# A bidirectional scan's two directions: added by VectorE for every head instead of by GpSimd for half of them and by TensorE for the rest

## The chip, the cores and the metric

One core of a Trainium2 chip runs the whole program in one launch. The metric is the device time of that launch in microseconds (us), the median of several runs. The engines are TensorE (PE in the profile, PEld for its weight loads), VectorE (DVE), ScalarE (ACT), GpSimd (POOL) and the DMA queue of SyncE (SP). They run side by side and wait for each other through semaphores.

## The reference, cut to what matters

Two layers of an encoder trunk on 512 positions of width 1024, in float32. The part that counts here is a Mamba-2 scan of 16 heads of width 64, run forwards and backwards in 4 chunks of 128 positions, the two directions summed:

```python
seg = a_cs[:, :, :, None] - a_cs[:, :, None, :]
decay = jnp.exp(jnp.where(lower, seg, -jnp.inf))
cb = jnp.einsum('bclgn,bcsgn->bclsg', Cc, Bc)
y_diag = jnp.einsum('bclsge,bcsgep->bclgep', cb[..., None] * decay, X)
...
y = y_fwd + y_bwd + d_skip.astype(f32)[:, None] * xs
```

For one head and one chunk, y_diag of both directions is (G_fwd + G_bwd) X, with G = cb * decay a 128x128 matrix for each direction and X (the head's 64 columns of inputs, 128 positions) the same in both. So the two matrices may be added first and multiplied once, or multiplied one by one into the same accumulator. Around the scan stand projections, attention, a short convolution and a gated feed-forward part.

## The kernel before, in words

Activations lie transposed, 128 features by 512 positions. Every weight matrix is cut into chunks of 128x1024, and each chunk becomes one tile of output in one of the eight PSUM banks. Float32 accuracy comes from a split: ScalarE writes a chunk's high part (L528), VectorE or GpSimd the low part, raw minus high (L834, L433), and TensorE makes three products a block (L1158 to L1160), 24 for a chunk. Raw, high and low parts have two buffers each. So chunk n+2 gets its high part when TensorE has used chunk n, then its low part, and its raw buffer is refilled by SP when that low part is done. TensorE starts chunk n+2 only when its whole low part is there.

The stage that the change touches is a list of slots written out by hand (SLOTS, L69): slots 0 to 11 are the short convolution's chunks, 12 to 19 the chunks of z (the gate), 20 to 27 the first half of the output projection. All engines go through the same list, each in its own order. In slot s TensorE first makes the tile of s and then the pieces of the scan that are due there; VectorE makes the low part of chunk s+2 (`low_after`, L829); in this stage all low parts are VectorE's. GROUP_AT, SEG_AT, WEIGH_AT and PAIR_AT (L112 to L115) say in which slot each piece of the scan is due; heads 0 to 7 have slots 3 to 12, heads 8 to 15 slots 14 to 23.

For a head h:

- SP copies 2x512 numbers to all partitions (`head_rows`, L350) into one of four buffers, `head_e(h)` = HEAD_E[h % 4]: two are in sb_e, one is sb_e_third, one is sb_squares. For h of 4 and more this waits for the products of the pair that used the buffer.
- VectorE subtracts a column, 8 instructions of 128x128 (`seg`, L905), ScalarE takes the exponential (L602), and VectorE multiplies both directions by CB from PSUM (`weigh`, L911, in slot WEIGH_AT). `g_done` counts these.
- For even h, GpSimd adds the second direction to the first (`add_directions`, L464); `gs_done` counts these.

Pair t is heads 2t and 2t+1, in slots 6, 8, 10, 12 and 17, 19, 21, 23. There TensorE makes `from_states` (L1336) and `within` (L1322): for an even head one product a chunk of positions, for an odd head two that accumulate, one for each direction. The even head's output goes to partitions 0 to 63 of a bank, the odd head's to 64 to 127. Before it TensorE waits for the even head's sum and for the odd head's `weigh`, which VectorE makes one slot earlier, in front of that slot's low part. In the pair's own slot VectorE combines the result behind its low part (`combine`, L915 to L923); SP's copies of the exponentials for the next pair (`pair_exps`, L370) and of the next heads' rows stand in the same queue as the weight loads (L333).

GpSimd has in this stage: the low part of the short convolution's output (L489, slots 2, 5, 8, 11), the scaled inputs of the states (L458), the adds of L464, the backward part (L468) and the gate (L473). A z tile is moved out of its bank by VectorE behind the slot's low part and `combine` (L1085), and TensorE's tile two slots later needs that bank.

Of the kernel before, what the change touches and what calls it, by code (L numbers as in the profile page):

```python
# [142 lines left out]
def build_trunk(nc, a):  # L143
# [18 lines left out]
    def sem(name, per=0):  # L162
        return Count(ctx.enter_context(nc.semaphore(name)), per, now)
# [68 lines left out]
    def bank(i):  # L232
# [43 lines left out]
    cb_mm, cb_done, xs_done, st_mm, sin_done = sem("cb_mm", 2), sem("cb_done", 4), sem("xs_done", 12), sem("st_mm", 12), sem("sin_done", 8)  # L276
    seg_done, e_done, g_done, y_mm = (
        sem(n, SSD_HEADS) for n in ("seg_done", "e_done", "g_done", "y_mm"))
    gs_done = sem("gs_done", SSD_HEADS // 2)
    yo_mm, y_read, t_read, z_copied, y_comb = (sem(n, 8) for n in ("yo_mm", "y_read", "t_read", "z_copied", "y_comb"))  # L280
    z_done = sem("z_done", 2)
    ff_tap, ff_silu, ff_hi, ff_lo = sem("ff_tap", 2 * FF_T), sem("ff_silu_done", FF_T), sem("ff_hi_done", FF_T), sem("ff_lo_done", FF_T)
# [8 lines left out]
    def head_e(h):  # L291

        return HEAD_E[h % 4]
# [130 lines left out]
    @block.gpsimd  # L424
    def _(pool):
        g = nc.gpsimd

        def w_low(n):
            pool.wait_ge(w_hi.handle, n + 1)
            if n % NCH == POS["dt", 0]:  # L430
                g.tensor_tensor(dt_parts(n, 1), dt_raw(n), dt_parts(n, 0).bitcast(F32), ALU.subtract).then_inc(w_lo.handle, 1)
                return
            g.tensor_tensor(WLO[:, n % 2, :], W[:, n % 2, :], WHI[:, n % 2, :].bitcast(F32), ALU.subtract).then_inc(w_lo.handle, 1)  # L433

        def low_after(kind, i):

            n = now[0] * NCH + POS[kind, i] + 2
            if (kind, i) == ("o2", 0):
                pool.wait_ge(w_lo.handle, n)
            if n < DEPTH * NCH:  # L440
                w_low(n)

        def sum_squares(grp):

            pool.wait_ge(*y_sq.at(4 * grp + 4))
            g.tensor_tensor(SQS[:, 0:2, :], SQS[:, 0:2, :], SQS[:, 2:4, :], ALU.add).then_inc(y_tree.handle, 1)
            pool.wait_ge(*y_tree.at(2 * grp + 1))
            g.tensor_tensor(SQS[:, 0, :], SQS[:, 0, :], SQS[:, 1, :], ALU.add).then_inc(y_tree.handle, 1)

        def scale_states(n):  # L450
            grp, j = n // 6, n % 6
            d, c = direction_chunk(j)
            col = column(d, 8 * grp)
            pool.wait_ge(*ws_done.at(1))
            pool.wait_ge(*tok_copied.at(5 * grp + 5))
            if j >= 2:
                pool.wait_ge(*st_mm.at(n - 1))
            g.tensor_tensor(SQ[:, j % 2, :].rearrange("p (h e) -> p h e", e=64), XT[:, c, :].rearrange("p (h e) -> p h e", e=64),  # L458
                            WS[:, c, col:col + 8].unsqueeze(2).to_broadcast([P, 8, 64]), ALU.mult).then_inc(xs_done.handle, 1)

        def add_directions(h):

            pool.wait_ge(*g_done.at(h + 1))
            g.tensor_tensor(head_e(h)[:, 0, :], head_e(h)[:, 0, :], head_e(h)[:, 1, :], ALU.add).then_inc(gs_done.handle, 1)  # L464

        def add_backward(t):
            pool.wait_ge(*y_read.at(t + 1))
            g.tensor_tensor(XC[:, t, 0:SEQ - P], XC[:, t, 0:SEQ - P], T[:, 1, 0:SEQ - P], ALU.add).then_inc(t_read.handle, 1)  # L468

        def gate(t):  # L470
            pool.wait_ge(*t_read.at(t + 1))
            pool.wait_ge(*z_done.at(t // 4 + 1))
            g.tensor_tensor(XC[:, t, :], XC[:, t, :], Z[:, t % 4, :], ALU.mult).then_inc(y_comb.handle, 1)  # L473

        w_low(0)
        w_low(1)
        for layer in range(DEPTH):
            now[0] = layer
            for pos in range(POS["sc", 0]):
                low_after(*CHUNKS[pos])  # L480
                if layer == 0 and CHUNKS[pos] == ("qk", 2):
                    pool.wait_ge(bias_row.handle, 2)
                    g.dma_start(scratch[:, :, :], rm["bias_row"][:, :].unsqueeze(1).to_broadcast([HEADS, COPIES, REL]))\
                        .then_inc(bias_stored.handle, 16)
            for s, (kind, i) in enumerate(SLOTS):
                if kind == "sc" and i % 3 == 2:
                    t = i // 3
                    pool.wait_ge(*sc_hi.at(t + 1))
                    g.tensor_tensor(rm["ml_sc"][:, t, :], SCP[:, :], rm["mh_sc"][:, t, :].bitcast(F32), ALU.subtract)\  # L489
                        .then_inc(sc_lo.handle, 1)  # L490
                for grp in range(SSD_GROUPS):
                    if 0 <= s - GROUP_AT[grp] < 3:
                        for j in range(2):
                            scale_states(6 * grp + 2 * (s - GROUP_AT[grp]) + j)
                if s in WEIGH_AT and WEIGH_AT[s] % 2 == 0:
                    add_directions(WEIGH_AT[s])
                if s in PAIR_AT:
                    add_backward(PAIR_AT[s])
                if s in (16, 17):
                    gate(2 * (s - 16))  # L500
                    gate(2 * (s - 16) + 1)
                if s in (20, 21, 22):
                    gate(s - 16)
                if s == 24:
                    gate(7)
                if s in (24, 27):
                    sum_squares((s - 24) // 3)
            for m in range(KT):
                low_after("o2", m)
            for j in range(2 * FF_T):  # L510
                low_after("up", j)
                if j % 2 == 1:
                    t = j // 2
                    pool.wait_ge(*ff_hi.at(t + 1))
                    g.tensor_tensor(FLO[:, t, :], FP[:, :], FHI[:, t, :].bitcast(F32), ALU.subtract).then_inc(ff_lo.handle, 1)  # L515
            for i in range(DOWN_C * KT):
                low_after("dn", i)
# [276 lines left out]
    def _(dve):  # L794
# [114 lines left out]
        def weigh(h):  # L909
            dve.wait_ge(*e_done.at(h + 1))  # L910
            v.tensor_tensor(head_e(h), head_e(h), CB[:, :, :], ALU.mult).then_inc(g_done.handle, 1)  # L911

        def combine(t):
            dve.wait_ge(*y_mm.at(2 * t + 2))
            step(v.scalar_tensor_tensor(XC[:, t, :], XC[:, t, :], par(PA_D + t), bank(6 + t % 2), ALU.mult, ALU.add))  # L915
# [26 lines left out]
        for layer in range(DEPTH):  # L942
# [81 lines left out]
            for s, (kind, i) in enumerate(SLOTS):  # L1024
# [41 lines left out]
                if s in WEIGH_AT:  # L1066
                    weigh(WEIGH_AT[s])
                low_after(kind, i)
                if s in PAIR_AT:
                    combine(PAIR_AT[s])  # L1070
                if kind == "sc" and i % 3 == 1:
# [75 lines left out]
    def _(pe):  # L1147
# [162 lines left out]

        def within(t):

            pe.wait_ge(*gs_done.at(t + 1))
            pe.wait_ge(*g_done.at(2 * t + 2))
            if t % 4 == 0:
                pe.wait_ge(*cb_done.at(2 * (t // 4) + 2))
            if t >= 2:
                pe.wait_ge(*y_read.at(t - 1))
            for c in range(QT):
                for h, d in ((2 * t, 0), (2 * t + 1, 0), (2 * t + 1, 1)):  # L1320
                    half = 64 * (h % 2)
                    ins = mm(BANK[half:half + 64, 6 + t % 2, P * c:P * c + P], XT[:, c, 64 * (h % 8):64 * (h % 8) + 64],  # L1322
                             head_e(h)[:, d, P * c:P * c + P], start=d == 0, stop=d == h % 2)
                    if c == QT - 1 and d == h % 2:
                        ins.then_inc(y_mm.handle, 1)

        def from_states(t):
# [231 lines left out]
```

## Time and profile before

| | us |
|---|---|
| median of 3 runs | 1656.96 |
| lowest, highest | 1655.63, 1657.75 |
| the profiled execution | 1656.37 |
| its span, first to last instruction | 1654.6 |
| TensorE matmul busy | 1634.1 (99%) |
| VectorE busy | 993.3 (60%) |
| GpSimd busy | 674.2 (41%) |
| ScalarE busy | 661.9 (40%) |

The granted TensorE clock is 1.000 on average over the span. "Busy" is time in which an engine had an instruction under way; matmuls overlap, so that their durations add up to more than the time that passes, and the distance from one start to the next says more. A row of a timeline has the start from the span's beginning, the duration, the engine, the source line, the operation, what it writes and reads, how many instructions are merged in the row and, in brackets, how long the engine was idle before it and what ended that. A float32 product is recorded as two passes, so that "x24" is 12 products.

### The profile page before, as it was taken

To read this page: it belongs to the slowest core of one execution; us is meant where nothing else is said; L and a number is where in the kernel's file an instruction comes from. 1 tells how busy PE (TensorE), PEld (TensorE's weight loads), DVE (VectorE), ACT (ScalarE), POOL (GpSimd) and SP (SyncE) were. 2 spreads that over 40 slices of the span, in tenths; PEclk is the share of its full clock that TensorE was granted. 3 is DMA by queue.
4 is the path that set the end of the run, shared out by engine and by line. 5 is a ranking of instruction groups with operands and counts; after the bars stand their busy time and mean duration, and the time that the engine had idled before them with its cause. 6 is when DMAs were issued, how large, how long until landed. Compare 5 with 4: busy or idle time off the path is not lost.

```text
span 1654.6 us, 20299 instructions
## 1 busy us (share of the span) xinstructions
PE 1634.1 (99%) x7864; PEld 1297.6 (78%) x7864; DVE 993.3 (60%) x1564; ACT 661.9 (40%) x916; POOL 674.2 (41%) x339
## 2 busy tenths in 40 slices
PE   7999999999999999999999999999999999999999
PEld 5777778877878888888877777787878788888887
DVE  4589869787764455522227898798887554554000
ACT  5455552335343333332244555523443433333221
POOL 3332222233445555554443222223244555555443
PEclk9999999999999999999999999999999999999999
DMA  5532135442222222222224221444522223222223
GB/s 170 139 91 74 60 117 146 134 146 94 90 90 99 93 91 100 89 92 96 92 90 127 87 74 62 124 146 130 149 95 90 90 89 100 92 91 98 95 92 109
DMA packets 57375, 170.93 MB, mean 103 GB/s; under 512 B 5984, under 2 KB 11872, under 8 KB 57280
## 3 DMA queue, kind: packets, MB, share of 16 engines
q1 hardware_dynamic: 56896, 168.88, 32.1%
q0 software_dynamic: 384, 0.75, 0.4%
q8 instruction: 63, 1.03, 0.3%
q14 instruction: 32, 0.26, 0.1%
HBM read 166.24 MB, written 3.38 MB: 103 GB/s over the span
## 4 chain that ended last, share of the span: by engine, by line
PE 92%; issue 2%; DVE 2%; POOL 1%; DMA 1%; ACT 1%; SPq 0%; DVEq 0%; POOLq 0%; ACTq 0%
PE banks L1158 27%; PE banks L1160 27%; PE banks L1159 27%; PE banks L1257 2%; PE banks L1236 2%; PE banks L1245 2%; PE banks L1322 1%; PE banks L1309 1%; PE banks L1336 1%; DMA sb_w_raw<-w_out 1%; PE banks L1216 1%; DVE sb_h_lo L809 0%; POOL sb_xc L473 0%; PE banks L1293 0%; DVE sb_squares L822 0%
## 5 line engine op out<-in xcount | busy, mean ns | idle before, releaser
L433 POOL TENSOR_TENSOR sb_w_lo<-sb_w_raw,sb_w_hi 128x1024 fp32r<-128x1024 f32 x200 | 482.4, 2412 | 634.9 <-ACT sb_w_hi L528 634.9
L1158 PE MATMUL banks<-sb_h_hi,sb_w_hi 128*128 128x512 f32 x1344 | 550.9, 410 | 11.3 <-POOL sb_w_lo L433 9.9
L528 ACT ACTIVATE sb_w_hi<-sb_w_raw 128x1024 fp32r<-128x1024 f32 x256 | 270.9, 1058 | 706.9 <-PE banks L1160 691.4
L1160 PE MATMUL banks<-sb_h_hi,sb_w_lo 128*128 128x512 f32 x1344 | 530.9, 395 | 0.0
L1159 PE MATMUL banks<-sb_h_lo,sb_w_hi 128*128 128x512 f32 x1344 | 530.6, 395 | 0.0
L1158 PEld LDWEIGHTS banks<-sb_h_hi,sb_w_hi 128*128 128x128 f32 x1344 | 253.5, 189 | 92.4 <-issue 34.7
L1159 PEld LDWEIGHTS banks<-sb_h_lo,sb_w_hi 128*128 128x128 f32 x1344 | 253.8, 189 | 60.9 <-issue 6.5
L1160 PEld LDWEIGHTS banks<-sb_h_hi,sb_w_lo 128*128 128x128 f32 x1344 | 253.5, 189 | 59.4
L1123 DVE TENSOR_TENSOR banks<-banks,sb_rstd 128x512 f32<-128x512 f32 x88 | 61.5, 699 | 145.3 <-PE banks L1160 135.7
L1160 PE MATMUL banks<-sb_ff_hi,sb_w_lo 128*128 128x512 f32 x352 | 138.9, 395 | 0.0
L1159 PE MATMUL banks<-sb_ff_lo,sb_w_hi 128*128 128x512 f32 x352 | 138.9, 395 | 0.0
L1158 PE MATMUL banks<-sb_ff_hi,sb_w_hi 128*128 128x512 f32 x352 | 138.9, 395 | 0.0
L1138 DVE TENSOR_TENSOR sb_x_stream<-banks,sb_x_stream 128x512 f32<-128x512 f32 x16 | 11.1, 692 | 199.2 <-PE banks L1160 199.2
L834 DVE TENSOR_TENSOR sb_w_lo<-sb_w_raw,sb_w_hi 128x1024 fp32r<-128x1024 f32 x56 | 82.1, 1465 | 19.4 <-ACT sb_w_hi L528 19.3
L1158 PEld LDWEIGHTS banks<-sb_ff_hi,sb_w_hi 128*128 128x128 f32 x352 | 66.3, 188 | 15.5
L1159 PEld LDWEIGHTS banks<-sb_ff_lo,sb_w_hi 128*128 128x128 f32 x352 | 66.3, 188 | 15.5
L1160 PEld LDWEIGHTS banks<-sb_ff_hi,sb_w_lo 128*128 128x128 f32 x352 | 66.3, 188 | 15.4
L515 POOL TENSOR_TENSOR sb_ff_lo<-sb_ff_prod,sb_ff_hi 128x512 fp32r<-128x512 f32 x44 | 57.0, 1296 | 51.4 <-DVE sb_ff_hi L1134 51.4
L857 DVE SCALAR_TENSOR_TENSOR sb_xc<-banks,sb_params,sb_xc 128x509 f32<-128x509 f32 (+2 forms) x96 | 71.9, 749 | 4.5 <-ACT sb_xc L585 1.7
L591 ACT ACTIVATE sb_probs<-sb_scores,sb_neg_max 128x512 f32<-128x512 f32 x64 | 45.7, 716 | 57.2 <-DVE sb_neg_max L883 57.2
L1125 DVE SCALAR_TENSOR_TENSOR sb_ff_val<-banks,sb_params,sb_ff_val 128x511 f32<-128x511 f32 x44 | 33.0, 749 | 46.3 <-ACT sb_ff_val L775 46.3
L1125 DVE SCALAR_TENSOR_TENSOR sb_ff_gate<-banks,sb_params,sb_ff_gate 128x511 f32<-128x511 f32 x44 | 33.0, 750 | 45.8 <-ACT sb_ff_gate L775 45.8
(202 smaller groups left out, 2255.9 us busy)
## 6 DMA issues: line engine op xcount, KB each, us to landing
sb_w_raw<-w_in SPq DMA_DIRECT2D x88, 512.0 KB, 3.4
sb_w_raw<-w_up SPq DMA_DIRECT2D x88, 512.0 KB, 3.3
sb_w_raw<-w_out SPq DMA_DIRECT2D x32, 512.0 KB, 3.3
sb_w_raw<-w_down SPq DMA_DIRECT2D x32, 512.0 KB, 3.3
sb_e<-sum_rows SPq DMA_DIRECT2D x16, 512.0 KB, 6.2
sb_bias_t<-bias_rows SPq DMA_DIRECT2D x16, 448.0 KB, 5.6
sb_exp_cs<-sum_rows SPq DMA_DIRECT2D x32, 192.0 KB
sb_w_raw<-w_down SPq DMA_DIRECT2D x16, 384.0 KB, 3.0
```

Source lines behind the costliest of these rows:

```text
L433: g.tensor_tensor(WLO[:, n % 2, :], W[:, n % 2, :], WHI[:, n % 2, :].bitcast(F32), ALU.subtract).then_inc(w_lo.handle, 1)
L515: g.tensor_tensor(FLO[:, t, :], FP[:, :], FHI[:, t, :].bitcast(F32), ALU.subtract).then_inc(ff_lo.handle, 1)
L528: sc.activation(WHI[:, n % 2, :], W[:, n % 2, :], ACT.Copy).then_inc(w_hi.handle, 1)
L591: sc.activation(PR[:, u % 4, :], S[:, u % 2, :], ACT.Exp, bias=NEGMAX[:, u % 4:u % 4 + 1], scale=-1.0, accum_out=DEN[:, u % 4:u % 4 + 1]). ...
L834: v.tensor_tensor(WLO[:, n % 2, :], W[:, n % 2, :], WHI[:, n % 2, :].bitcast(F32), ALU.subtract).then_inc(w_lo.handle, 1)
L857: ins = v.scalar_tensor_tensor(acc[:, lo:hi], src[:, lo + o:hi + o], par(PA_CONV7 + 8 * n + t), acc[:, lo:hi], ALU.mult, ALU.add)
L1123: v.tensor_tensor(bank(b), bank(b), RSTD, ALU.mult).then_inc(up_scaled.handle, 1)
L1125: step(v.scalar_tensor_tensor(acc[:, 1:SEQ], BANK[:, b, 0:SEQ - 1], par(col), acc[:, 1:SEQ], ALU.mult, ALU.add))
L1158: mm(out, whi, hhi, start=start, stop=False)
L1159: mm(out, whi, hlo, start=False, stop=False)
L1160: return mm(out, wlo, hhi, start=False, stop=stop)
L1236: ins = mm(bank(2 + u % 2), qs[hs, h // 2, P * qt:P * qt + P], ks[hs, h // 2, :], start=n == 0, stop=n == 2)
```

## The change

VectorE adds the two directions of every head, even and odd, in one instruction each, right behind the low part of the slot in which it weighs that head. GpSimd no longer adds. TensorE makes one product for each head and chunk of positions, and waits for the sums of both heads of a pair. `gs_done` counts 16 a layer instead of 8.

```diff
-    gs_done = sem("gs_done", SSD_HEADS // 2)
+    gs_done = sem("gs_done", SSD_HEADS)
...
@@ GpSimd
-        def add_directions(h):
-
-            pool.wait_ge(*g_done.at(h + 1))
-            g.tensor_tensor(head_e(h)[:, 0, :], head_e(h)[:, 0, :], head_e(h)[:, 1, :], ALU.add).then_inc(gs_done.handle, 1)
-
...
-                if s in WEIGH_AT and WEIGH_AT[s] % 2 == 0:
-                    add_directions(WEIGH_AT[s])
@@ VectorE
+        def add_directions(h):
+
+            dve.wait_ge(*g_done.at(h + 1))
+            v.tensor_tensor(head_e(h)[:, 0, :], head_e(h)[:, 0, :], head_e(h)[:, 1, :], ALU.add).then_inc(gs_done.handle, 1)
+
...
                 if s in WEIGH_AT:
                     weigh(WEIGH_AT[s])
                 low_after(kind, i)
+                if s in WEIGH_AT:
+                    add_directions(WEIGH_AT[s])
                 if s in PAIR_AT:
                     combine(PAIR_AT[s])
@@ TensorE
         def within(t):
 
-            pe.wait_ge(*gs_done.at(t + 1))
-            pe.wait_ge(*g_done.at(2 * t + 2))
+            pe.wait_ge(*gs_done.at(2 * t + 2))
...
             for c in range(QT):
-                for h, d in ((2 * t, 0), (2 * t + 1, 0), (2 * t + 1, 1)):
+                for h in (2 * t, 2 * t + 1):
                     half = 64 * (h % 2)
                     ins = mm(BANK[half:half + 64, 6 + t % 2, P * c:P * c + P], XT[:, c, 64 * (h % 8):64 * (h % 8) + 64],
-                             head_e(h)[:, d, P * c:P * c + P], start=d == 0, stop=d == h % 2)
-                    if c == QT - 1 and d == h % 2:
+                             head_e(h)[:, 0, P * c:P * c + P], start=True, stop=True)
+                    if c == QT - 1:
                         ins.then_inc(y_mm.handle, 1)
```

## Rows read from the trace of the kernel before

**Rows 1.** The page, busy time of each engine (share of span, instructions).
```profile
PE 1634.1 (99%) x7864; PEld 1297.6 (78%) x7864; DVE 993.3 (60%) x1564; ACT 661.9 (40%) x916; POOL 674.2 (41%) x339
```

**Rows 2.** Busy time by stretch: PE, PEld, DVE, ACT, POOL, granted clock, DMA.
```profile
247.30:263.90 16.60, 16.60 (x90) 13.02 (x88) 16.39 (x25) 5.45 (x6) 5.90 (x4) 1.00 0.28 81
```

**Rows 3.** Timeline of TensorE, first products of pairs, the tiles behind.
```profile
262.03 1.97 PE L1322 MATMUL banks<-sb_e,sb_x_tok 128*64 128x128 f32 x24
263.93 0.50 PE L1158 MATMUL banks<-sb_h_hi,sb_w_hi 128*128 128x512 f32 x1
...
276.64 0.32 PE L1322 MATMUL banks<-sb_e_third,sb_x_tok 128*64 128x128 f32 x1
...
291.22 1.97 PE L1322 MATMUL banks<-sb_e,sb_x_tok 128*64 128x128 f32 x24
...
306.32 0.29 PE L1322 MATMUL banks<-sb_e_third,sb_x_tok 128*64 128x128 f32 x1 [0.42 <-issue]
...
360.45 0.32 PE L1322 MATMUL banks<-sb_e_third,sb_x_tok 128*64 128x128 f32 x1
...
369.04 0.47 PE L1158 MATMUL banks<-sb_mh_at,sb_w_hi 128*128 128x512 f32 x1 [0.84 <-DVE sb_z L1085]
...
391.97 0.29 PE L1322 MATMUL banks<-sb_e_third,sb_x_tok 128*64 128x128 f32 x1 [1.20 <-issue]
```

**Rows 4.** Timeline of TensorE, attention's P x V and the product behind.
```profile
180.17 1.09 PE L1257 MATMUL banks<-sb_probs_t,sb_v 128*64 128x128 f32 x16
181.20 0.50 PE L1158 MATMUL banks<-sb_h_hi,sb_w_hi 128*128 128x512 f32 x1
```

**Rows 5.** Timeline of VectorE, two operands in SBUF.
```profile
256.49 0.69 DVE L937 TENSOR_TENSOR sb_t_normed<-sb_s_in,sb_decays 128x512 f32<-128x512 f32 x1
...
299.42 0.56 DVE L923 TENSOR_TENSOR sb_xc<-sb_xc,sb_t_normed 128x384 f32<-128x384 f32 x1
```

**Rows 6.** Timeline of GpSimd, and VectorE's instructions beside and without it.
```profile
251.34 2.21 POOL L464 TENSOR_TENSOR sb_e<-sb_e 128x512 f32<-128x512 f32 x1 [1.63 <-DVE sb_e L911]
252.32 2.57 DVE L1076 SCALAR_TENSOR_TENSOR sb_sc_acc<-sb_sc_cx,sb_params,sb_sc_acc 128x511 f32<-128x511 f32 x2
...
274.71 1.53 DVE L1076 SCALAR_TENSOR_TENSOR sb_sc_acc<-sb_sc_cx,sb_params,sb_sc_acc 128x511 f32<-128x511 f32 x2
...
281.85 1.82 POOL L489 TENSOR_TENSOR sb_ml_sc<-sb_sc_prod,sb_mh_sc 128x512 fp32r<-128x512 f32 x1 [11.80 <-ACT sb_mh_sc L699]
283.63 1.29 POOL L464 TENSOR_TENSOR sb_e<-sb_e 128x512 f32<-128x512 f32 x1
...
295.20 2.35 DVE L834 TENSOR_TENSOR sb_w_lo<-sb_w_raw,sb_w_hi 128x1024 fp32r<-128x1024 f32 x1
...
306.39 2.09 POOL L489 TENSOR_TENSOR sb_ml_sc<-sb_sc_prod,sb_mh_sc 128x512 fp32r<-128x512 f32 x1 [4.88 <-ACT sb_mh_sc L699]
```

**Rows 7.** Timeline of VectorE, low parts of slots 5 to 22.
```profile
261.61 2.05 DVE L834 TENSOR_TENSOR sb_w_lo<-sb_w_raw,sb_w_hi 128x1024 fp32r<-128x1024 f32 x1
...
273.57 1.22 DVE L834 TENSOR_TENSOR sb_w_lo<-sb_w_raw,sb_w_hi 128x1024 fp32r<-128x1024 f32 x1
...
281.29 1.23 DVE L834 TENSOR_TENSOR sb_w_lo<-sb_w_raw,sb_w_hi 128x1024 fp32r<-128x1024 f32 x1 [0.90 <-ACT sb_w_hi L528]
...
289.95 1.22 DVE L834 TENSOR_TENSOR sb_w_lo<-sb_w_raw,sb_w_hi 128x1024 fp32r<-128x1024 f32 x1
...
305.01 1.21 DVE L911 TENSOR_TENSOR sb_squares<-sb_squares,banks 128x1024 f32<-128x1024 f32 x1
306.13 1.22 DVE L834 TENSOR_TENSOR sb_w_lo<-sb_w_raw,sb_w_hi 128x1024 fp32r<-128x1024 f32 x1
...
357.34 1.22 DVE L834 TENSOR_TENSOR sb_w_lo<-sb_w_raw,sb_w_hi 128x1024 fp32r<-128x1024 f32 x1
...
364.64 1.23 DVE L834 TENSOR_TENSOR sb_w_lo<-sb_w_raw,sb_w_hi 128x1024 fp32r<-128x1024 f32 x1 [1.57 <-ACT sb_w_hi L528]
...
391.79 1.22 DVE L834 TENSOR_TENSOR sb_w_lo<-sb_w_raw,sb_w_hi 128x1024 fp32r<-128x1024 f32 x1
```

## The prediction

> **What bounds the kernel now.** I read the page first: TensorE is busy for 99% of the span, VectorE for 60%, GpSimd for 41% [rows 1]. Taken alone that says that only TensorE's work counts. The change lies in 22 of the 28 scan slots of each layer, so I read the busy time by stretch next. From slot 5's tile to the end of pair 0's products VectorE is busy for 16.39 of 16.60 us [rows 2]: in this stage it is as full as TensorE, and the 60% is an average over other stages. Then I read TensorE's timeline around the products of each pair [rows 3]: it already stands still before pair 3 (0.42 us) and pair 7 (1.20), put down to "issue" though a VectorE product ends just before (306.22 against 306.32 at pair 3 [rows 3, 7]), and before slot 21's tile (0.84, for VectorE's z). Last the timelines of VectorE and GpSimd, for when each low part ends and what holds it [rows 6, 7]. All times are of layer 1; layer 2 repeats each of these rows 818.2 us later, and the rows of layer 1 stand for both.
>
> **TensorE's part.** A pair has 12 products, recorded as 24 passes, and from their first start to the next tile's it takes 263.93 - 262.03 = 1.90 us [rows 3]. The change leaves 8 products, 16 passes. Nearest row: the attention's P x V, also 128x64 weights against 128 columns, also 16 passes that alternate between the two halves of the bank's partitions, takes 181.20 - 180.17 = 1.03 us [rows 4]. The bounds are an equal share of the 12 (4/12 of 1.90, 0.63) and nothing. I take 0.87, since that row is the same instruction in the same order: 16 pairs, 13.9 us, if nothing else waits.
>
> **VectorE's part.** It gets 16 adds a layer, 32 in all, of two 128x512 operands in SBUF. Nearest row: L937, two SBUF inputs, 128x512, 0.69 us. Lower bound: L923, 384 columns, 0.56 [rows 5]. Instructions here start 0.08 before the one in front ends (low ends 274.79, L1076 starts 274.71 [rows 6, 7]), so an add delays what is behind it by 0.6 and ends 0.6 behind the low. It may be dearer: VectorE and GpSimd hold each other up when both use SBUF operands. L1076 takes 2.57 beside GpSimd's add at 251.34, 1.53 without; a low 2.35 instead of 1.22 (295.20); and GpSimd's L489 takes 1.82 and 2.09, having first to wait for the low in front of it and then running for 1.2 [rows 5 to 7]. Instructions that read PSUM are not held. So an add can cost from 0.5 to 0.6 + 1.2.
>
> The add's own wait, for the product one low part earlier, is over when it comes: nothing. Behind it in VectorE's queue stand the combining of a pair, the taps and the next head's subtractions.
>
> **GpSimd's part.** It loses 8 adds a layer, 1.29 us when not held (283.63) [rows 6]. No wait of TensorE but that of the products ends on them, so they are worth only what they held of VectorE: 1.04 (L1076), 1.13 (low), and by the same pattern 0.4 (L923 behind the add at 283.63) and about 1.3 in heads 8 to 15: 3.9 a layer, against 16 x 0.6 = 9.6 added.
>
> The Trainium skill, GPSIMD Engine Reference, Engine selection, says to put an elementwise add on VectorE, as GpSimd is about twice as slow with two inputs. The trace agrees on the ratio (0.69 against 1.29), and by this rule, which asks only which engine is quicker, the sum would be TensorE's 13.9 alone. It leaves out who waits behind the quicker engine.
>
> **The new wait, pair by pair.** Both heads' adds must now be done, and the odd head's stands behind the slot's low. I carry two lags: D of TensorE, V of VectorE.
> - Pair 0. Add 0 is +0.6, the freed L1076 -1.0: V -0.4. The low ends 263.66 - 0.4, add +0.6, and 0.1 to TensorE (as from 306.22 to 306.32): 264.0 against 262.03. Wait 1.9, D = 1.9 - 0.87 = 1.0.
> - Pair 1. Adds 1, 2: V 0.8. Ready 274.79 + 0.8 + 0.7 = 276.3, TensorE at 276.64 + 1.0: no wait, D 0.2. Pairs 4 and 6 stand like this one.
> - Pair 2. Add 3: V 1.4. VectorE's idle 0.90 at 281.29 [rows 7] takes back part, but what it waits for, a weight load, is queued on SP behind a copy that waits for pair 0's products, 1.0 later: V 1.0. Behind that low GpSimd's L489 already waits, so it goes first: add 4 costs 1.2 + 0.6, less L923's 0.4: V 2.4. Ready 291.17 + 2.4 + 0.7 = 294.3 against 291.22 + 0.2: wait 2.9, D 2.2.
> - Pair 3. Add 5, the freed low (-1.1), add 6: V 2.5. Behind the low (ends 307.35) L489 waits again (306.39): ready 307.35 + 2.5 + 1.2 + 0.7 = 311.7 against 306.32 + 2.2: wait 3.2, D 4.5.
> - In slots 12 to 15 VectorE waits for TensorE, so V becomes D. Pair 4: D 3.6.
> - Pair 5. Adds 8 to 10 less 1.3 freed: V 5.0. Ready 358.56 + 5.0 + 0.7 = 364.3 against 360.45 + 3.6: wait 0.2, D 3.0.
> - Slot 21's tile waits for z. Add 11 gives 5.6, the idle 1.57 at 364.64 takes 1.6 back, add 12: V 4.6, so D 4.6.
> - Pair 6: D 3.7. Pair 7: V 4.6 and add 14, 5.2: ready 393.01 + 5.2 + 0.7 = 398.9 against 391.97 + 3.7: wait 3.2, D 6.1.
> The waits come to 13.0 a layer (slot 21's 1.6 among them), the shorter products to 7.0. The rest, 6.1, is lost, as TensorE has no idle time afterwards to make it up: 12.2 in two layers. The profiled execution took 1656.37 (its span 1654.6 and 1.8 around it; the median of the runs is 0.6 above it): 1656.4 + 12.2 = 1668.6, and I write 1668.
>
> **Rivals.**
> - GpSimd doesn't get in ahead of adds 4 and 7 (the copy that it waits for may come later than the add). Pair 2 then waits 1.7 and pair 3 2.0: 3.8 a layer, 1664. For it: an order of tenths of a microsecond decides. Against: in both rows L489 was issued before the low ended. Chance 0.17.
> - Dearer than the walk: the products get no shorter, or an add takes 0.8. With products of 1.90 pair 7 alone is 6.9 late, and 7.8 with the loads that follow later: 1670 to 1672; adds of 0.8 put 3.2 a layer more on V, and nearly all of that on D: 1674. Against: rows 4, 5. Chance 0.12.
> - Faster, at the products of pairs 0, 3 and 7: the add ends before TensorE gets there. It decides where GpSimd's absence gives VectorE more back than its adds take, 9.6 a layer. With adds that cost nothing pair 7's products would still start behind their low, 1.1 later than now, less the 1.3 that heads 8 to 15 get back: with the 0.87 of the pair itself 1.1 a layer gained, 1654. With no wait at all it is 1642.5. For it: 3.9 of the 9.6 is in the rows, and VectorE idles in slots 12 to 15. Against: it has 0.2 us idle before pair 0. Chance 0.08.
> The end of 1642.5 is what the Trainium skill's rule above (GPSIMD Engine Reference, Engine selection) comes to.
> - The two cancel, within 0.2% (3.3 us, about what a measurement can tell here): waits of under 8.6 a layer. Chance 0.05.
> - The forecast, 1665 to 1671: 0.58.
>
> **How the numbers follow.** The likeliest case gives 1668. The range leaves out faster, same, and what lies beyond the dear end: 1660 to 1674; it takes in GpSimd's order (1664), adds of 0.5 (1665) and of 0.8, and longer products (1672). Slower: 0.58 + 0.17 + 0.12 = 0.87, same 0.05, faster 0.08.
>
> **What would show it.** TensorE's products of a pair in 1.0 to 1.1 us with 16 passes. Idle or "issue" before them of about 2 us at pair 0, 3 at pairs 2, 3 and 7, none at 1, 4 and 6. Adds of 0.69, two of them a layer near 1.9 or begun late behind L489. VectorE's busy time up by some 18 us (32 x 0.69 less what was held), GpSimd's down by 28. TensorE's idle before slot 21 over 2 us. It is wrong if the products start when they did, if their 1.90 stays, or if the lag of layer 1 is made up in the feed-forward part. A fall of the granted clock, 1.00 in this stage so far [rows 2], during the longer waits would make it slower than I say.

## The result and the profile after

| | before | after |
|---|---|---|
| median of 5 runs, us | 1656.96 | 1670.44 |
| lowest, highest | 1655.63, 1657.75 | 1669.77, 1671.76 |
| profiled execution, its span | 1656.37, 1654.6 | 1671.40, 1669.3 |
| mean granted clock | 1.000 | 0.994 |

The ratio is 1.0084, with a 95% interval of 1.0072 to 1.0095: 13.5 us slower. The forecast was 1668 (1660 to 1674).

The page of the kernel after, busy time of each engine; it answers to [rows 1].

```profile
PE 1628.1 (98%) x7736; PEld 1289.7 (77%) x7736; DVE 1005.2 (60%) x1596; ACT 661.2 (40%) x916; POOL 644.2 (39%) x323
```

TensorE has 6.0 us less to do and still ends 14.7 later (span against span): what it saved and more turned into waiting. The waits of TensorE give the place. The view, of the whole span, has the waiting operation, what it waited for, us in total, times, longest.

```profile
PE banks L1321 <- DVE sb_squares L909: 10.9, 4, 4.4
PE banks L1321 <- DVE sb_e L909: 9.6, 4, 3.2
PE banks L1158 <- DVE sb_z L1085: 4.3, 2, 2.1
```

L1321 is the pair's products, L909 the new adds. Eight waits are the pairs 0, 2, 3 and 7 of two layers; pairs 1, 4, 5 and 6 have none. The timeline of TensorE in layer 1 shows them one by one, and answers to [rows 3] (the line numbers are lower here: L1335 is from_states, L1321 within).

```profile
249.68 0.80 PE L1158 MATMUL banks<-sb_h_hi,sb_w_hi 128*128 128x512 f32 x1
...
262.94 1.50 PE L1335 MATMUL banks<-sb_bc,sb_s_in 128*128 128x128 f32 x12
266.22 1.09 PE L1321 MATMUL banks<-sb_e,sb_x_tok 128*64 128x128 f32 x16 [1.78 <-DVE sb_e L909]
267.25 0.50 PE L1158 MATMUL banks<-sb_h_hi,sb_w_hi 128*128 128x512 f32 x1
...
296.91 1.97 PE L1321 MATMUL banks<-sb_e,sb_x_tok 128*64 128x128 f32 x16 [3.16 <-DVE sb_e L909]
298.81 0.80 PE L1158 MATMUL banks<-sb_h_hi,sb_w_hi 128*128 128x512 f32 x1
...
314.03 0.32 PE L1321 MATMUL banks<-sb_e_third,sb_x_tok 128*64 128x128 f32 x1 [1.94 <-DVE sb_squares L909]
...
375.41 0.47 PE L1158 MATMUL banks<-sb_mh_at,sb_w_hi 128*128 128x512 f32 x1 [2.13 <-DVE sb_z L1085]
...
400.62 0.47 PE L1321 MATMUL banks<-sb_e_third,sb_x_tok 128*64 128x128 f32 x1 [4.36 <-DVE sb_squares L909]
```

Read three things. Slot 5's tile starts at 249.68, 2.3 later than in [rows 2]: this execution was already late before the change acts, so 2.3 is taken off every time below. Pair 0 shows the product time forecast: 267.25 - 266.22 = 1.03. Pair 2, with the same 16 passes, shows 298.81 - 296.91 = 1.90. The busy time by stretch says why (columns as in [rows 2]; the last three are of the tile behind pair 7, and of pairs 2 and 7 in layer 2):

```profile
292.20:296.90 4.70, 1.55 (x13) 1.32 (x12) 4.17 (x8) 2.00 (x2) 0.00 (x0) 0.96 0.24 80
296.90:298.80 1.90, 1.89 (x16) 1.57 (x16) 1.90 (x9) 0.34 (x1) 0.00 (x0) 0.50 0.83 271
394.80:400.60 5.80, 1.46 (x13) 1.27 (x11) 5.28 (x11) 4.08 (x6) 0.62 (x1) 0.86 0.01 4
400.60:402.50 1.90, 1.88 (x16) 1.57 (x16) 1.90 (x3) 1.13 (x2) 0.00 (x0) 0.50 0.74 229
402.50:409.70 7.20, 7.20 (x27) 5.76 (x26) 3.46 (x6) 0.00 (x0) 4.15 (x3) 0.77 0.33 85
1122.00:1124.00 2.00, 1.67 (x16) 1.40 (x16) 2.00 (x10) 0.12 (x1) 0.00 (x0) 0.64 0.68 224
1225.20:1230.00 4.80, 3.93 (x29) 3.23 (x30) 4.73 (x8) 1.98 (x3) 0.00 (x0) 1.00 0.49 129
```

Behind the waits of 3.16 and 4.36 us the granted clock stands at 0.50, the 1.2 GHz level, where the stage was at 1.00 before [rows 2]. The products that the change made shorter then take as long as the longer ones did. Layer 2 is not the same in this: behind pair 2's wait (2.86) the clock fell again, behind pair 7's (2.81) it did not.

VectorE and GpSimd at pairs 2 and 3, against [rows 6, 7]: the low part, the add behind it, and GpSimd's L484 beside it.

```profile
285.06 1.23 DVE L827 TENSOR_TENSOR sb_w_lo<-sb_w_raw,sb_w_hi 128x1024 fp32r<-128x1024 f32 x1 [0.95 <-ACT sb_w_hi L521]
286.20 1.78 DVE L909 TENSOR_TENSOR sb_e<-sb_e 128x512 f32<-128x512 f32 x1
...
296.17 0.68 DVE L909 TENSOR_TENSOR sb_e<-sb_e 128x512 f32<-128x512 f32 x1
...
311.09 1.22 DVE L827 TENSOR_TENSOR sb_w_lo<-sb_w_raw,sb_w_hi 128x1024 fp32r<-128x1024 f32 x1
312.23 1.75 DVE L909 TENSOR_TENSOR sb_squares<-sb_squares 128x512 f32<-128x512 f32 x1
```

```profile
285.63 1.81 POOL L484 TENSOR_TENSOR sb_ml_sc<-sb_sc_prod,sb_mh_sc 128x512 fp32r<-128x512 f32 x1 [12.46 <-ACT sb_mh_sc L692]
...
311.35 2.08 POOL L484 TENSOR_TENSOR sb_ml_sc<-sb_sc_prod,sb_mh_sc 128x512 fp32r<-128x512 f32 x1 [4.88 <-ACT sb_mh_sc L692]
```

L484 was issued while the low part ran, goes next, and the add comes third: 1.78 and 1.75 instead of 0.68. The Trainium skill, SBUF — State Buffer, SBUF: two separate sides, says that a VectorE operation with two inputs in SBUF and a GpSimd operation that reads SBUF share one port, and that the one that starts first keeps it for its whole instruction. The trace agrees (L484 took 1.81 and 2.08, where 1.27 is what it takes when nothing holds it), and adds the order of a third that is already waiting.

Lag of TensorE, that is how many us later than in the kernel before it starts, in layer 1, at the tile that follows (2.3 taken off; the last column is experiment e5 less its own 1.2):

| behind | forecast | after | e5 |
|---|---|---|---|
| pair 0 | 1.0 | 1.0 | 1.0 |
| pair 1 | 0.2 | 0.1 | 0.1 |
| pair 2 | 2.2 | 3.4 | 1.6 |
| pair 3 | 4.5 | 4.5 | 3.6 |
| pair 4 | 3.6 | 3.6 | 2.7 |
| pair 5 | 3.0 | 2.7 | 1.9 |
| slot 21's wait | 4.6 | 4.0 | 3.2 |
| pair 6 | 3.7 | 3.2 | 2.3 |
| pair 7 | 6.1 | 6.3 | 4.6 |

Behind pair 7 another 1.4 is lost in the tile at half clock. Layer 1 ends 7.5 late, layer 2 adds 4.9, and 2.3 + 7.5 + 4.9 = 14.7, the difference of the spans.

### The profile page after: what moved, and what is told of

Same layout as the page of the kernel before. It is cut to its first block, busy times and chain, and to the rows that moved or that the text cites. A ratio compares the mean times of both kernels' runs of the same rounds, so it can differ in the third digit from the quotient of the medians.

```text
span 1669.3 us, 20055 instructions
## 1 busy us (share of the span) xinstructions
PE 1628.1 (98%) x7736; PEld 1289.7 (77%) x7736; DVE 1005.2 (60%) x1596; ACT 661.2 (40%) x916; POOL 644.2 (39%) x323
## 3 DMA queue, kind: packets, MB, share of 16 engines
q8 instruction: 62, 1.02, 0.3%
## 4 chain that ended last, share of the span: by engine, by line
PE 83%; DVE 9%; issue 3%; ACT 3%; DMA 2%; SPq 0%; POOL 0%; DVEq 0%; ACTq 0%
PE banks L1158 25%; PE banks L1160 24%; PE banks L1159 24%; PE banks L1257 2%; DMA sb_w_raw<-w_in 2%; PE banks L1236 2%; PE banks L1245 2%; DVE sb_squares L898 1%; DVE sb_w_lo L827 1%; PE banks L1216 1%; DVE sb_e L898 1%; DVE sb_t_normed L920 1%; DVE sb_e L909 1%; PE banks L1309 1%; PE banks L1321 0%
## 5 line engine op out<-in xcount | busy, mean ns | idle before, releaser
L1158 PE MATMUL banks<-sb_h_hi,sb_w_hi 128*128 128x512 f32 x1344 | 552.3, 411 | 13.3 <-POOL sb_w_lo L433 11.9
L827 DVE TENSOR_TENSOR sb_w_lo<-sb_w_raw,sb_w_hi 128x1024 fp32r<-128x1024 f32 x56 | 74.7, 1333 | 17.7 <-ACT sb_w_hi L521 17.7
L463 POOL TENSOR_TENSOR sb_xc<-sb_xc,sb_t_normed 128x384 f32<-128x384 f32 x16 | 18.9, 1179 | 135.7 <-DVE sb_xc L921 135.7
```

Of the source, the lines that this page charges most:

```text
L827: v.tensor_tensor(WLO[:, n % 2, :], W[:, n % 2, :], WHI[:, n % 2, :].bitcast(F32), ALU.subtract).then_inc(w_lo.handle, 1)
L1158: mm(out, whi, hhi, start=start, stop=False)
```

## The experiments

The theory: a pair's products start when VectorE's stream (its instructions in their order) gets to the last add, so what counts is how much VectorE has to do before that and what stands between; the clock's falls come on top. Rivals: GpSimd's hold-ups are the loss; or only the new wait is, wherever VectorE has time; or only the amount of work. All ratios are against runs of the kernel before beside them (medians 1656.1 to 1656.7).

**e1, twelve products again.** The one part undone that was meant to gain. The odd heads' second direction is counted twice, so the sums are not the reference's; only the time is used.

```diff
-                for h in (2 * t, 2 * t + 1):
+                for h, d in ((2 * t, 0), (2 * t + 1, 0), (2 * t + 1, 1)):
```

> Kernel after, but TensorE makes 12 products a pair again (the second direction of the odd head a second time, so the odd heads' backward part counts twice); the adds and waits stay. Theory (VectorE's stream behind the slot's low part says when a pair's products start): the longer products mostly fill time in which TensorE would wait for VectorE anyway. In the walk by rows the lag of a layer grows from about 5.6 us to 7.7, so 4 us more than the kernel after, 1675 (1672 to 1677); less if shorter waits also spare TensorE the half clock. Rival (the shorter products are worth their full 0.87 us a pair): 16 x 0.87 = 14 us more, 1684.

1677.35 us, ratio 1.0127 (1.0112 to 1.0143). The shorter products are worth 6.9 us here (7.8 if each kernel is taken against its own runs of the kernel before), half of their 13.9: the rest was waiting anyway. It is 0.35 above the theory's range; the longer waits and the clock (mean 0.995) are still there.

**e2, GpSimd adds both heads.**

```diff
+                if s in WEIGH_AT:
+                    add_directions(WEIGH_AT[s])   # in GpSimd's list, taken out of VectorE's
```

> Kernel after with its 8 products, but GpSimd makes the adds of both heads and VectorE makes none. Theory: TensorE now waits for GpSimd's add of the odd head (1.3 us and behind the low part of the same slot that holds GpSimd up), and the adds hold VectorE's operations up in turn: by the walk 5 to 7 us a layer over the kernel before, 1668 to 1672, about as slow as the kernel after, with waits before the products of pairs 0 to 3 that end on GpSimd. Rival (what costs is VectorE's own time for 16 adds a layer): without them VectorE is as in the kernel before and the shorter products count, 1657 - 14 plus the wait for the odd head's add, 8 pairs x 2 x 0.6 = 10: 1653 or less than 1657.

1674.07 us, ratio 1.0106 (1.0090 to 1.0121), 2 us above the theory's range and far from the rival. Waits of TensorE in layer 1, and one of GpSimd's adds:

```profile
PE banks L1321 <- POOL sb_squares L464: 6.9, 3, 3.2
PE banks L1321 <- POOL sb_e L464: 5.2, 2, 2.7
```

```profile
266.43 2.21 POOL L464 TENSOR_TENSOR sb_e_third<-sb_e_third 128x512 f32<-128x512 f32 x1 [0.68 <-DVE sb_e_third L911]
```

The same wait, on another engine: 12.1 us in five waits. Most of GpSimd's adds take 2.2 and not 1.29, beside the low part that follows the product on VectorE. So VectorE's own 16 adds are not needed for the loss: with none of them on VectorE the kernel is as slow.

**e3 and e5, fillers for the clock.** Products of constants run on TensorE while it would wait, into the bank that the pair's own products overwrite. In e3 they are 512 columns wide, at pairs 2 and 7 alone; in e5 128 wide, at pairs 0, 2, 3 and 7.

```diff
             if t >= 2:
                 pe.wait_ge(*y_read.at(t - 1))
+            for _ in range({0: 6, 2: 10, 3: 11, 7: 13}.get(t, 0)):
+                mm(BANK[:, 6 + t % 2, 0:P], con["ident"], CON[:, 0, :], start=True, stop=True)
+            pe.wait_ge(*gs_done.at(2 * t + 2))
```

> Kernel after, with filler products on TensorE (4 of 512 columns before pair 2, 5 before pair 7, into the bank that the pair's own products then overwrite) that run while TensorE would wait for the adds. Theory (the half clock after the longest waits is what the kernel after lost beyond the walk of the prediction): the granted clock stays at 2.4 GHz behind pairs 2 and 7, their products take 1.03 instead of 1.90 and the tile behind pair 7 some 5.7 instead of 7.1: 2 to 3 us less than the kernel after, 1667.5 to 1668.5. Rival (the clock falls for another reason, or what it costs is taken up by later waits): within 1 us of 1670.4.

e3: 1670.85 us, ratio 1.0089 (1.0074 to 1.0104), the same as the kernel after. That looked like the rival, but its stretches show that in layer 1 the fall had moved, from pair 2 to behind pair 3:

```profile
296.20:297.30 1.10, 1.10 (x18) 0.92 (x17) 1.10 (x6) 0.17 (x1) 0.00 (x0) 1.00 0.86 320
313.10:316.40 3.30, 3.30 (x20) 2.58 (x17) 2.45 (x4) 0.00 (x0) 0.00 (x0) 0.50 1.00 243
```

And pair 2's filler, 0.90 for each product, ended late: the add was done at 295.53 (294.84 + 0.69), the pair's products start at 296.21.

> Kernel after with short filler products on TensorE (128x128 against 128 columns; 6 before pair 0's own products, 10 before pair 2, 11 before pair 3, 13 before pair 7), some 0.22 us each as worked out from the fillers of four times the width in the run before, so that they end before the adds do. Theory (the clock's falls behind the waits cost 2 to 4 us of the kernel after; the first filler took 0.9 us each, ended with or after the adds and left pairs 0 and 3 bare, so the falls only moved there): the products start as in the kernel after, the granted clock stays at 2.4 GHz behind them, 1667 to 1668.5. Rival (the falls cost nothing in the end): 1670 to 1671.

e5: 1666.01 us (1665.69 to 1666.39), ratio 1.0057 (1.0042 to 1.0072), mean clock 1.000. Its timeline of TensorE:

```profile
292.42 2.40 PE L1318 MATMUL banks<-sb_constants 128*128 128x128 f32 x20
294.86 1.09 PE L1323 MATMUL banks<-sb_e,sb_x_tok 128*64 128x128 f32 x16
...
308.48 2.62 PE L1318 MATMUL banks<-sb_constants 128*128 128x128 f32 x22
311.99 0.32 PE L1323 MATMUL banks<-sb_e_third,sb_x_tok 128*64 128x128 f32 x1 [0.89 <-DVE sb_squares L909]
...
394.06 3.07 PE L1318 MATMUL banks<-sb_constants 128*128 128x128 f32 x26
398.58 0.32 PE L1323 MATMUL banks<-sb_e_third,sb_x_tok 128*64 128x128 f32 x1 [1.46 <-DVE sb_squares L909]
```

The fillers hold nothing up: they end before the add does, or at pair 2 0.02 us behind it (294.82 against 294.80). No idle time in front of the products is over 1.5 us (slot 21's 2.1 stays), and pair 2's products take 1.02 again. Work that computes nothing makes the kernel 4.4 us faster than the change alone (3.9 if each is taken against its own runs of the kernel before), 1 us more than the theory's range allows. The remaining 9.6 is waiting, less the shorter products.

Not all of the 4.4 is the half clock. The two profiled executions are 5.0 apart. Of this 1.2 is there before the stage. Behind pair 7 of layer 1 it is 2.2: 0.87 in the products and 1.4 in the tile, both at half clock. And 1.6 (0.9 in layer 1, 0.7 in layer 2) comes from pair 2's slot, whose low part has its weights earlier in e5 than in the kernel after, at a clock of 1.00 in both (262 to 292, 1076 to 1112). In layer 1 of e5 VectorE makes it at once, without the 0.95 of idle time in front:

```profile
283.01 1.22 DVE L827 TENSOR_TENSOR sb_w_lo<-sb_w_raw,sb_w_hi 128x1024 fp32r<-128x1024 f32 x1
```

Whether the fillers or chance moved that load isn't shown. The slow products of pair 2 themselves cost nothing in the end: pair 3's products wait for VectorE in both runs, and in layer 1 they start 0.88 earlier in e5 (start of the stage taken off), which is the load's 0.9.

**e4, the adds without the wait.** The kernel before, and VectorE adds two idle tiles behind each low part of the 16 slots.

```diff
                 low_after(kind, i)
+                if s in WEIGH_AT:
+                    idle_add(WEIGH_AT[s])      # 128x416, read by nobody
```

> Kernel before with all its waits, 12 products and GpSimd's adds, and on VectorE, behind the low part of each of the 16 slots a layer, one more add (128x416, about 0.57 us) into a tile that nobody reads. No product waits for it. Theory (VectorE's stream is full in this stage, so that its time counts wherever it stands): most of 16 x 0.5 us appears at TensorE in each layer, 6 to 11 us a layer, 1670 to 1679. Rival (VectorE has idle time, 60% busy; only the wait of the products for the adds costs): within 2 us of 1657.

1677.71 us, ratio 1.0127 (1.0111 to 1.0144): 21.6 us slower though no product waits for an add. The group of the adds, from the grouped lines (busy us, mean ns):

```profile
L918 DVE TENSOR_TENSOR sb_spare<-sb_rstd 128x416 f32<-128x416 f32 x32 | 38.4, 1200 | 0.0
```

The rival with the free 40% of VectorE falls. But the experiment is dearer than meant: GpSimd's adds are still there and hold these, so that one takes 1.20 us and not 0.57. It shows that time in this place of VectorE's stream reaches TensorE, 21.6 for 38.4 us, and not what 16 x 0.6 would cost; the clock's falls are in it (mean 0.996).

**e6, the adds in front of the low part.**

```diff
                     weigh(WEIGH_AT[s])
+                    add_directions(WEIGH_AT[s])
                 low_after(kind, i)
-                if s in WEIGH_AT:
-                    add_directions(WEIGH_AT[s])
```

> Kernel after with the add of every head in front of the slot's low part on VectorE instead of behind it. Theory (the amount of VectorE's work is what is short, its order only moves the loss): the products of pairs 0 and 1 start earlier by up to 1 us, but every tile's low part comes 0.6 later and slot 21's tile and pair 7 stand as before: 1669 to 1674. Rival (the place behind the low part, and GpSimd getting in between low part and add at pairs 2 and 3, is what costs): the waits of pairs 0, 2, 3 and 7 shrink by 1.1 to 2.3 us each, 12 us in two layers, 1658 to 1661.

1669.96 us, ratio 1.0083 (1.0068 to 1.0098): no better, and the rival's 1658 to 1661 falls. TensorE's waits in layer 1:

```profile
PE banks L1320 <- DVE sb_squares L909: 4.1, 2, 2.2
PE banks L1157 <- DVE sb_w_lo L827: 2.7, 2, 1.6
PE banks L1157 <- DVE sb_z L1084: 2.6, 1, 2.6
```

The products wait less, and the tiles wait for their low part and for z instead. Order alone moves the loss.

**e7 and e8, half of the subtraction on ScalarE.** Of `seg`'s 8 operations ScalarE makes the second direction's 4, in the kernel before (e7) and after (e8).

```diff
-            for d in range(2):
-                for c in range(QT):
+            for c in range(QT):                        # VectorE: direction 0
...
+            for c in range(QT):                        # ScalarE: direction 1
+                sc.activation(head_e(h)[:, 1, at], head_e(h)[:, 1, at], ACT.Relu, bias=AS[:, c, column(1, h):column(1, h) + 1], scale=-1.0)
+            sc.activation(head_e(h)[:, 1, :], head_e(h)[:, 1, :], ACT.Exp, scale=-1.0)
```

> Kernel before, but of each head's subtraction and clamp (8 VectorE operations of 128x128, 0.20 us apart) ScalarE makes the second direction's four (as relu of the negated difference, and the exponential with a negated scale). VectorE loses 0.8 us a head, 16 heads a layer; ScalarE gets some 1.4 a head. Theory (VectorE's stream is the limit at pairs 3 and 7 and at slot 21 already in the kernel before): those waits of 0.4, 0.8 and 1.2 us and the loads late behind them go, 1 to 3 us a layer, 1650 to 1655. Rival (TensorE at 99% is the only bound): 1656 or more, with ScalarE's longer chain to the exponentials making it slower.

e7: 1653.18 us, ratio 0.9980 (0.9971 to 0.9989). The waits at pairs 3 and 7 are gone but for 0.2: the kernel before was already short of VectorE there.

> Kernel after with the same part of the subtractions on ScalarE, so that VectorE gives back 0.8 us a head where the change gives it 0.6. Theory: nearly the whole loss goes; by the walk a layer comes out between 1.5 us below and 0.5 above the kernel before, 1653 to 1658 (the products of pairs 0, 2 and 3 still wait 1 to 2 us behind their low part). Rival (the added wait of the products, not VectorE's amount of work, costs): above 1664.

e8: 1664.28 us (1660.85 to 1667.48), ratio 1.0045 (1.0030 to 1.0059). A miss of over 6 us, and at the rival's figure. Two rows of its VectorE, in front of pair 7:

```profile
382.50 1.22 DVE L913 TENSOR_TENSOR sb_e_third<-sb_e_third,banks 128x1024 f32<-128x1024 f32 x1 [4.25 <-ACT sb_e_third L605]
...
388.47 3.73 DVE L907 TENSOR_SCALAR sb_squares<-sb_squares,sb_small 128x128 f32<-128x128 f32 x4
```

VectorE stands idle for 4.25 us for head 14's exponential, which ScalarE makes behind its silu, and then needs 3.73 for four subtractions beside GpSimd's backward add and gate. So free time doesn't help where the chain of one slot (exponential, product, low part, add) is late. That is one pair; the waits at pairs 0, 2, 3 and 7 all stay, 16.4 us in two layers against 20.5 in the kernel after, and so do falls of the clock (mean 0.996). That place counts as well as amount is a reading of this, which e9 to e12 try.

**e9 to e12, the whole subtraction on ScalarE.** 13 heads of 16 wholly, heads 0 and 10 by half, head 14 (behind the silu) on VectorE. e12 is the kernel before with that, e9 the kernel after with it, e10 puts the odd head's add in front of the low part and the even head's behind it, e11 leaves the even head's on GpSimd.

```diff
+            if h in SCALAR:                            # e9 to e12, on ScalarE
+                for d in range(2):
+                    for c in range(QT):
+                        sc.activation(head_e(h)[:, d, at], head_e(h)[:, d, at], ACT.Relu, bias=AS[:, c, column(d, h):column(d, h) + 1], scale=-1.0)
+                sc.activation(head_e(h), head_e(h), ACT.Exp, scale=-1.0)
...
# e10, on VectorE
                     weigh(WEIGH_AT[s])
+                    if WEIGH_AT[s] % 2:
+                        add_directions(WEIGH_AT[s])
                 low_after(kind, i)
-                if s in WEIGH_AT:
+                if s in WEIGH_AT and WEIGH_AT[s] % 2 == 0:
                     add_directions(WEIGH_AT[s])
```

> Kernel after (adds of both heads behind the low part, 8 products), with the whole subtraction of 13 of the 16 heads of a layer on ScalarE (8 relus of 128x128, some 0.32 us apart, and one exponential), of heads 0 and 10 the second direction, and head 14 wholly on VectorE. VectorE gives back 1.6 us a head against the 0.6 of the adds. Theory (VectorE's amount of work in front of the products is what the change ran out of): the waits of pairs 0, 2, 3 and 7 shrink to under 1 us where VectorE isn't waiting for ScalarE, and the shorter products show: 1646 to 1654. Rival (the place of the add behind the low part costs whatever VectorE has to do; relief of 0.8 a head bought only 3 us a layer): 1658 to 1662.

e9: 1652.71 us, ratio 0.9975 (0.9965 to 0.9984).

> The run beside this one (whole subtractions on ScalarE), but the odd head's add, which is the one the pair's products wait for, stands in front of the slot's low part, and the even head's behind it. Theory: with VectorE relieved and the last add 1.2 us earlier all waits of the products but those of pairs 3 and 7 go: 2 to 4 us less than with both behind, 1642 to 1650, faster than both kernels. Rival (the low part, now 0.6 later in every second slot, makes the tiles wait instead): no better than the run beside it.

e10: 1649.32 us, ratio 0.9954 (0.9939 to 0.9969).

> As the run beside this one (odd head's add in front of the low part on VectorE), but the even head's add stays on GpSimd as in the kernel before. Theory: the even head's add is never late, so GpSimd can keep it; it holds VectorE up now and then by 1 us where VectorE's own add would take 0.6, so within 2 us of the run beside it, 1642 to 1651. Rival (GpSimd's hold-ups of VectorE are what cost): over 3 us slower than it.

e11: 1647.08 us, ratio 0.9943 (0.9927 to 0.9960): 9.6 us faster than the kernel before and 23 faster than the change as it was made.

> Kernel before (12 products, even adds on GpSimd, none on VectorE) with the same whole subtractions on ScalarE as in the last three runs. It says what the relief is worth without the change. Theory: TensorE had no waits left in the scans once 0.8 us a head was gone (1653.2 with waits of 0.3 at pair 7 and 0.5 at slot 21), so double the relief adds at most 1 us: 1651 to 1653.5; the odd head's add and the shorter products on top of it are then worth 4 to 6 us more (1647.1 with the even add on GpSimd). Rival (the relief itself made the last kernels fast, and the shorter products add nothing): 1647 to 1649.

e12: 1652.16 us, ratio 0.9974 (0.9965 to 0.9984).

Set e12 beside the others. The relief alone is worth 4 us. The change as it was made, on top of it, is worth nothing (1652.71 against 1652.16), though VectorE gives back 1.6 a head for 0.6: its products still wait at pair 3. With the add that the products wait for in front of the low part, and the other one off VectorE, the same change is worth 5 us. The first product of pair 3 in e9 and in e11:

```profile
307.05 0.32 PE L1343 MATMUL banks<-sb_e_third,sb_x_tok 128*64 128x128 f32 x1 [2.87 <-DVE sb_squares L931]
```

```profile
305.84 0.29 PE L1351 MATMUL banks<-sb_e_third,sb_x_tok 128*64 128x128 f32 x1 [1.41 <-issue]
```

What stands in front of it in e9, the low part and the add of VectorE, and in e11 the add alone:

```profile
304.35 2.04 DVE L849 TENSOR_TENSOR sb_w_lo<-sb_w_raw,sb_w_hi 128x1024 fp32r<-128x1024 f32 x1
306.32 0.68 DVE L931 TENSOR_TENSOR sb_squares<-sb_squares 128x512 f32<-128x512 f32 x1
```

```profile
304.34 1.40 DVE L938 TENSOR_TENSOR sb_squares<-sb_squares 128x512 f32<-128x512 f32 x1
```

In e9 GpSimd's short-convolution operation (L489) holds the low part (2.04 instead of 1.22) and the add comes behind it; in e11 the same operation holds the add (1.40 instead of 0.68), and the products start 1.2 earlier. The clock has a part in the difference too: e9's ten runs had means of 0.996 to 0.999, and the time goes with it (1655.72 at 0.996, 1650.61 at 0.999), while e11 and e12 stay at 0.999 and above; e10's four go from 1646.04 at 0.999 to 1652.31 at 0.997. Amount and place are both needed in what was run; neither e6 (place) nor e9 (amount) alone brings the shorter products out. e11's arrangement without the relief by ScalarE was not run, so how far it alone would go is open.

## Why the prediction was right

**TensorE's part.** 16 passes in 1.03, as taken from [rows 4], at 13 of the 16 pairs. Right, though the bounds that stand beside it (a gain of 0.63, and nothing) don't hold the 0.87 that was taken. At pairs 2 and 7 of layer 1 it was 1.90 and at pair 2 of layer 2 1.73, at the lower clock. (The 22 slots in which the change is said to lie are 18 by WEIGH_AT and PAIR_AT; no term hangs on it.)

**VectorE's part.** An add is 0.68 alone. The forecast of its busy time, +18, was too high: +11.9 (1005.2 against 993.3). It was not the sum of its own terms either: 32 x 0.69 less 7.8 is 14.3. The adds are 26.1 us in sum; as each starts 0.08 before the one in front ends, they put on about 23.5 (an estimate), so some 11.6 was given back over the whole span, where the prediction counted 3.9 a layer, 7.8. The low parts alone, here in the kernel before and after, give back 7.4:

```profile
L834 DVE TENSOR_TENSOR sb_w_lo<-sb_w_raw,sb_w_hi 128x1024 fp32r<-128x1024 f32 x56 | 82.1, 1465 | 19.4 <-ACT sb_w_hi L528 19.3
```

```profile
L827 DVE TENSOR_TENSOR sb_w_lo<-sb_w_raw,sb_w_hi 128x1024 fp32r<-128x1024 f32 x56 | 74.7, 1333 | 17.7 <-ACT sb_w_hi L521 17.7
```

**GpSimd's part.** 30.0 less, 28 forecast. That L489 (now L484) goes ahead of adds 4 and 7 was right in both places, in both layers, and with that the rival of 1664 fell.

**The walk.** Waits at pairs 0, 2, 3 and 7 and in front of slot 21, none at 1, 4 and 6: as forecast. Product starts, 2.3 added to the forecast: pair 0 266.3 against 266.22, pair 2 296.6 against 296.91, pair 3 314.0 against 314.03, pair 7 401.2 against 400.62. Pair 5 needed no wait; it was put at 0.2.

The single waits are less exact: 1.94 at pair 3 and 4.36 at pair 7, where 3.2 was forecast for both; their sum in layer 1 is 13.4 for 13.0.

**What the walk had wrong.** That the total came so near is in part luck: two errors of about 2 us cancelled. The clock's fall stood in the text as a risk and not in the sum; in this execution it costs 2.2, the products and the tile of pair 7 in layer 1. The other falls cost nothing in the end, as the next products wait for VectorE anyway. And the walk's V was too large. It can be read from the starts of VectorE's products with CB (L911 before, L904 after), less what the layer began late (2.3 and 9.9; 1.2 in e5):

| V at the product of | forecast | after, layer 1 | after, layer 2 | e5, layer 1 |
|---|---|---|---|---|
| head 1 | -0.4 | -0.4 | -0.4 | -0.4 |
| head 4 | 1.4 | 1.4 | 1.4 | 1.4 |
| head 5 | 2.4 | 2.7 | 2.4 | 1.9 |
| head 7 | 2.5 | 2.6 | 2.3 | 1.7 |
| head 8 | 4.5 | 4.5 | 4.2 | 3.6 |
| head 11 | 5.0 | 4.5 | 4.2 | 3.6 |
| head 15 | 5.2 | 4.6 | 4.2 | 3.7 |

Up to head 4 every term of V holds. Between heads 4 and 5 stands the load of pair 2's slot. In e1 and in layer 2 of the kernel after it leaves V at 2.4, as in the walk; it came 0.3 later in layer 1 of the kernel after and 0.5 sooner in e5. The term that was mis-sized in all three is what heads 8 to 15 get back from GpSimd's absence: 1.3 in the walk, but 1.8 in the runs, as three adds of 0.6 leave V at head 11 where it was at head 8 (layer 1, the kernel before and after):

```profile
333.28 1.21 DVE L911 TENSOR_TENSOR sb_e<-sb_e,banks 128x1024 f32<-128x1024 f32 x1
...
356.20 1.22 DVE L911 TENSOR_TENSOR sb_squares<-sb_squares,banks 128x1024 f32<-128x1024 f32 x1 [1.13 <-ACT sb_squares L602]
```

```profile
340.11 1.21 DVE L904 TENSOR_TENSOR sb_e<-sb_e,banks 128x1024 f32<-128x1024 f32 x1
...
363.02 1.22 DVE L904 TENSOR_TENSOR sb_squares<-sb_squares,banks 128x1024 f32<-128x1024 f32 x1 [1.13 <-ACT sb_squares L595]
```

The rest of layer 2's difference, 0.3 at head 8, is there from pair 3 on. Without the fall at pair 7 layer 1 would have ended 5.3 late, and layer 2 ended 4.9 late, where 6.1 was forecast for each. By terms: 12.2, less 2.0 for V, plus 2.2 for the clock, is 12.4, which the spans show (14.7 less the late start of 2.3). 1668.6 plus that 0.2, the 2.3 and the 0.3 by which the time outside the span was longer is the profiled 1671.4; the median lies 1.0 below.

**The rule on engines.** The prediction set against itself the Trainium skill, GPSIMD Engine Reference, Engine selection: give the elementwise add to VectorE, the quicker engine. By row the ratio holds (0.68 against 1.29), and still the fastest kernel here, e11, leaves half of the adds on GpSimd (2.2 us ahead of e10 with all of them on VectorE, though the two intervals overlap and e10's clock fell more).

**Faster and same.** The rival that VectorE gets more back than it gives put 1654 on adds that cost nothing behind the low part. In e9, where VectorE is relieved by more than the adds take, 1652.7 was measured; as the relief alone is worth 4 us (e12), that nearness doesn't test the rival's sum. Its point of decision holds: with the adds behind the low part the shorter products brought nothing there.

**Open.** Why the profiled execution was 2.3 late before the stage began wasn't settled (from 20 to 30 us its granted clock was 0.83, in e5 and in the kernel before 1.00; its first waits for low parts were 2.0 longer than before), nor why e5's load in front of pair 2's low part came sooner. The shares given for the 4.4 are those of two profiled executions; the other runs have no profile.

## What to carry to other kernels

A busy share of 60% over the whole span hides a stage in which the engine is full: read it by stretch, and walk the stream in front of the wait that the change adds. When work moves to such an engine, first make room there (here ScalarE had it: 44% busy after taking the subtractions), and put the one instruction that the critical engine waits for in front of work that is not awaited yet. Place alone left the loss as it was (e6), and room alone left the change worth nothing (e9 against e12). A wait on TensorE can cost more than its length, through the clock; but slow work costs only where the next start doesn't wait for another engine anyway.

## What the runs showed of the hardware

- Waits of 3.16 and 4.36 us in a stage that had none over 1.20 before were followed by stretches at 1.2 GHz, in which 16 passes took 1.90 instead of 1.03. The length of the wait alone doesn't say it: in layer 2 a wait of 2.86 was followed by such a stretch and one of 2.81 was not. Filler products that replaced the idle time kept the clock at 1.00; fillers at two of four places let it fall behind a third (e3).
- A VectorE add behind a low part waited for a GpSimd operation issued during that low part: 1.75 to 1.78 against 0.68; with adds of both engines in each slot the mean was 1.20 for 128x416 (e4), and GpSimd's own rose from 1.29 to 2.2 (e2).
- Eight ScalarE activations of 128x128 with a bias column, back to back, in e9:

```profile
296.08 2.44 ACT L609 ACTIVATE sb_squares<-sb_squares,sb_small 128x128 f32<-128x128 f32 x8
```

  0.31 each, against 0.20 on VectorE when nothing holds it (eight in 1.66, L898 in the kernel after). None was held by GpSimd: the mean is 0.39 of overlapping time in every group of e9, where VectorE's four took 3.73 (e8).
